# Two transformer blocks on one core: the turn of neighbourhood probabilities one round later, with four probability buffers

## The reference

```
o_a = _gqa_blocked(q_a, k_a, v_a) * jax.nn.silu(g_a)
o_b = _neighbourhood_attn(q_b, k_b, v_b, na_rpb[l])
o_b = o_b * jax.nn.silu(g_b)
mixed = jnp.concatenate([o_a, o_b], axis=-1)
x = x + mixed @ w_out[l]
...
sc = jnp.where(mask, sc + bias.astype(jnp.float32), -jnp.inf)
p = jax.nn.softmax(sc, axis=(-2, -1)).astype(v.dtype)
o = jnp.einsum('bhjqkc,bkjchd->bjqhd', p, v_band)
```

## Time and profile before

| | |
|---|---|
| median of three executions | 2462.85 us (2457.55 to 2464.51) |
| the profiled execution's own time | 2464.41 us |
| its span, first to last instruction | 2462.4 us |
| PE busy | 2380.6 us, 97% |
| DVE busy | 1711.4 us, 70% |
| ACT busy | 1122.1 us, 46% |
| POOL busy | 523.2 us, 21% |
| A steps (first to last `exp` of kind A) | 2043.3 to 2216.5 us |
| B steps (first to last `exp` of kind B) | 2218.9 to 2351.5 us |

### The profile page before, as it was taken

How to read it: one execution, slowest core, us unless ns; L and a number is a source line. 1 busy time by engine, 2 the same in 40 slices (tenths; PEclk the granted TensorE clock), 3 DMA queues, 4 the chain that set the end, 5 groups by cost and what they waited for, 6 DMA issues and landing times.

```text
span 2462.4 us, 32578 instructions
## 1 busy us (share of the span) xinstructions
PE 2380.6 (97%) x11129; PEld 1925.2 (78%) x11129; DVE 1711.4 (70%) x2762; ACT 1122.1 (46%) x1950; POOL 523.2 (21%) x453
## 2 busy tenths in 40 slices
PE   7999999899999999999999899999999999999998
PEld 2578888688878888878888688888888897886677
DVE  7788877788786664277766877785641227998863
ACT  3455455444434223245455544342421127887851
POOL 0211001333232000210100432320110003557731
PEclk9999999999999999999999999998999999999999
DMA  8726665654434731235643754440453472336521
GB/s 322 274 90 212 231 215 200 232 184 154 134 102 142 265 111 75 97 115 181 208 167 116 268 186 126 156 129 18 173 141 122 150 184 73 98 97 171 154 69 69
DMA packets 272970, 382.23 MB, mean 155 GB/s; under 512 B 63665, under 2 KB 173361, under 8 KB 272818
## 3 DMA queue, kind: packets, MB, share of 16 engines
q1 hardware_dynamic: 272818, 380.27, 47.3%
HBM read 279.54 MB, written 106.70 MB: 157 GB/s over the span
## 4 chain that ended last, share of the span: by engine, by line
PE 80%; DVE 9%; issue 5%; POOL 3%; ACT 2%; SPq 1%; DMA 1%; DVEq 0%; POOLq 0%; ACTq 0%
PE banks L2761 22%; PE banks L2762 22%; PE banks L2763 22%; PE banks L2831 2%; PE banks L3307 2%; PE banks L3325 2%; POOL probs L1492 1%; DVE neg_max L2698 1%; DVE stage L2060 1%; PE banks L2779 1%; POOL X L1524 1%; PE banks L3294 1%; PE banks L3295 1%; SPq L1303 1%; DVE X L2437 1%
## 5 line engine op out<-in xcount | busy, mean ns | idle before, releaser
L2761 PE MATMUL banks<-Hhi,Whi 128*128 128x512 f32 x1760 | 696.4, 396 | 25.1 <-DVE X L2437 13.9
L2762 PE MATMUL banks<-Hlo,Whi 128*128 128x512 f32 x1760 | 687.6, 391 | 0.0
L2763 PE MATMUL banks<-Hhi,Wlo 128*128 128x512 f32 x1760 | 687.5, 391 | 0.0
L2761 PEld LDWEIGHTS banks<-Hhi,Whi 128*128 128x128 f32 x1760 | 332.1, 189 | 106.7 <-issue 24.3
L2762 PEld LDWEIGHTS banks<-Hlo,Whi 128*128 128x128 f32 x1760 | 332.3, 189 | 69.9 <-issue 2.4
L2763 PEld LDWEIGHTS banks<-Hhi,Wlo 128*128 128x128 f32 x1760 | 331.9, 189 | 70.3
L2761 PE MATMUL banks<-T,Whi 128*128 128x512 f32 x720 | 283.7, 394 | 6.7 <-DVE Wlo L2353 6.7
L2763 PE MATMUL banks<-T,Wlo 128*128 128x512 f32 x720 | 283.0, 393 | 0.0
L2762 PE MATMUL banks<-T,Whi 128*128 128x512 f32 x720 | 283.0, 393 | 0.0
L1696 ACT ACTIVATE Whi<-stage 128x512 fp32r<-128x512 f32 (+2 forms) x180 | 104.9, 584 | 229.4 <-PE banks L2763 229.2
L2437 DVE SCALAR_TENSOR_TENSOR X<-banks,mod,X 128x512 f32<-128x512 f32 x180 | 134.3, 746 | 98.9 <-PE banks L2763 97.5
(11 more groups left out here) (258 smaller groups left out, 4082.1 us busy)
## 6 DMA issues: line engine op xcount, KB each, us to landing
stage<-w SPq DMA_DIRECT2D x58, 1024.0 KB, 6.4
stage<-hidden SPq DMA_DIRECT2D x224, 256.0 KB, 3.6
hidden<-slot SPq DMA_DIRECT2D x196, 256.0 KB, 2.1
stage<-ada_t SPq DMA_DIRECT2D x36, 1024.0 KB, 5.3
x_saved<-X SPq DMA_DIRECT2D x32, 512.0 KB, 4.5
stage<-w_in SPq DMA_DIRECT2D x13, 1024.0 KB, 6.2
stage<-ada_w SPq DMA_DIRECT2D x12, 1024.0 KB, 7.3
X<-x_saved SPq DMA_DIRECT2D x24, 512.0 KB, 4.9
```

The lines of the kernel that those rows point to most:

```text
L2761: nc.tensor.matmul(out_bank, whi, xhi, start=start, stop=False, skip_group_check=onto)
L2762: nc.tensor.matmul(out_bank, whi, xlo, start=False, stop=False, skip_group_check=onto)
L2763: return nc.tensor.matmul(out_bank, wlo, xhi, start=False, stop=stop, skip_group_check=onto)
```

## The change

In the B steps, `turn` and everything behind it (`probs_hi`, `probs_lo`, `outputs`, `lower_half`, `whole_output`, `gated`) works one round later; `delayed` gives the tile. Kind A keeps its lags. At the change from A to B, round 3 has no turn. B's probabilities get four buffers, `near_probs`, so that `exp` of tile u waits for the turn of u-4; the pads behind them are zeroed four times and not twice. In B, DVE takes `row_maxima` ahead of `invert_sum`. The mask's thirds move from rounds 5, 6, 7 to 3, 6, 7 and, within B, from 13, 14, 15 to 12, 14, 15. `OT` becomes two buffers behind the two biases, `biased` moves behind the new buffers, and `attend_end` writes out the longer tail. SP's code is unchanged.

```diff
-    SC = sb("biased", [P, 2, NI], at=t_at + 8 * S)
     PE_ = sb("probs", [P, 2, S], at=t_at)
+    PB = sb("near_probs", [P, 4, NI + HD], at=t_at)
+    SC = sb("biased", [P, 2, NI], at=t_at + 16 * (NI + HD))
...
+    def delayed(u, lag, kind, before):
+        old, new = u - lag - (before == "B"), u - lag - (kind == "B")
+        return ([(old, before)] if before and old < 0 else []) + ([(new, kind)] if new >= 0 else [])
...
+    def freed(u, kind, first):
+        if kind == "B":
+            return (-2 if u == 0 else 0) if first and u < 4 else 2 * u - 6
+        return 2 * u - 2
...
-                    if kind == "B" and u in (5, 6, 7):
-                        mask_bias(T, 1, u - 5)
-                    if (kind == "B") != last and u in (13, 14, 15):
-                        mask_bias(T, 0, u - 13, ahead=1)
-                    for w, k in lagged(u, 9, kind, before):
+                    if kind == "B" and u in (3, 6, 7):
+                        mask_bias(T, 1, (3, 6, 7).index(u))
+                    rounds = (12, 14, 15) if kind == "B" else (13, 14, 15)
+                    if (kind == "B") != last and u in rounds:
+                        mask_bias(T, 0, rounds.index(u), ahead=1)
+                    for w, k in delayed(u, 9, kind, before):
...
-                reach(act, t_ready, T("v2", 2 * u - 2))
+                reach(act, t_ready, T("v2", freed(u, kind, first)))
...
-                    for w, k in lagged(u, 8, kind, before):
+                    for w, k in delayed(u, 8, kind, before):
                         if w % 4 == 3:
                             lower_half(T, w // 4)
-                    for w, k in lagged(u, 3, kind, before):
+                    for w, k in delayed(u, 3, kind, before):
                         probs_hi(T, w, k)
...
-                    for w, k in lagged(u, 2, kind, before):
-                        invert_sum(T, w)
+                    if kind == "A":
+                        for w, k in lagged(u, 2, kind, before):
+                            invert_sum(T, w)
                     for w, k in lagged(u, 1, kind, before):
                         row_maxima(T, w, k, width(k, w))
-                    for w, k in lagged(u, 3, kind, before):
+                    if kind == "B":
+                        for w, k in lagged(u, 2, kind, before):
+                            invert_sum(T, w)
+                    for w, k in delayed(u, 3, kind, before):
                         probs_lo(T, w, k)
...
-                    for w, k in lagged(u, 3, kind, before):
+                    for w, k in delayed(u, 3, kind, before):
-                        turn(T, w, k, zeroed=w + 1 if kind == "B" and before == "A" and 0 <= w < 2 else 0)
+                        turn(T, w, k, zeroed=w + 1 if kind == "B" and before == "A" and 0 <= w < 4 else 0)
                     scores(T, u, kind, width(kind, u), before)
-                    for w, k in lagged(u, 7, kind, before):
+                    for w, k in delayed(u, 7, kind, before):
                         outputs(T, w, k, zeroed=6 * (w // 4 + 1) if kind == "B" and before == "A" and 0 <= w < 8 else 0)
```

More of the change, by code:

```diff
@@ L395, in build @@
     PTl = sb("PTl", [P, 2, QT, H], F32R, at=h_at + 4 * KT * S)
-    OT = sb("OT", [P, 2, H], at=acc_at - 7 * S // 2)
+    OT = [sb(f"OT{i}", [P, H], at=w_at + 4 * UNIT * (spare + 2 * i) + 4 * (NF + NI)) for i in range(2)]
     OS = sb("OS", [P, 2, H], at=acc_at + S // 2)
@@ L1490, in scale @@
                 pool.sem_inc(sums_seen, 1)
-                row = PE_[:, u % 2, 0:width(kind, u)]
+                row = probs(u, kind)[:, 0:width(kind, u)]
                 nc.gpsimd.tensor_scalar(out=row, in0=row, scalar1=rden[:, u % 4:u % 4 + 1], scalar2=1.0,
@@ L1527, in attend @@
                 for u in range(PAIR):
-                    if u % 4 == 1:
-                        reach(pool, mixed_done, T("vg", (u - 9) // 4))
+                    for w, k in delayed(u, 10, kind, before):
+                        if w % 4 == 3:
+                            reach(pool, mixed_done, T("vg", w // 4 + 1))
                     for w, k in lagged(u, 2, kind, before):
                         scale(T, w, k)
-                    if kind == "B" and before == "A" and u < 2:
+                    if kind == "B" and before == "A" and u < 4:
                         zero_pad(T, u)
@@ L1980, in silu, with exp @@
                         vals(T, 0, P, P, range(4 * i, 4 * i + 4))
-            def exp(T, u, kind, n):
+            def exp(T, u, kind, n, first=False):
                 act.wait_ge(max_done, T("v", u + 1))
-                reach(act, t_ready, T("v2", 2 * u - 2))
+                reach(act, t_ready, T("v2", freed(u, kind, first)))
                 scores = SB_[:, 2 * (u % 2):2 * (u % 2) + 2, :].rearrange("p b n -> p (b n)")[:, 0:n]
@@ L1987, in exp @@
                     scores = SC[:, u % 2, 0:n]
-                nc.scalar.activation(PE_[:, u % 2, 0:n], scores, ACT.Exp, bias=neg_max[:, u % 4:u % 4 + 1],
+                nc.scalar.activation(probs(u, kind)[:, 0:n], scores, ACT.Exp, bias=neg_max[:, u % 4:u % 4 + 1],
                                      scale=-1.0 if kind == "B" else 1.0,
@@ L2003, in lower_half @@
                 reach(act, os_done, T("vg", g - 1))
-                nc.scalar.activation(OT[0:HD, g % 2, :], OB[HD:P, g % 2, :], ACT.Copy).then_inc(ot_done, 1)
+                nc.scalar.activation(OT[g % 2][0:HD, :], OB[HD:P, g % 2, :], ACT.Copy).then_inc(ot_done, 1)
             def attend(T, kind, i, before, last):
                 for u in range(PAIR):
-                    for w, k in lagged(u, 8, kind, before):
+                    for w, k in delayed(u, 8, kind, before):
                         if w % 4 == 3:
                             lower_half(T, w // 4)
-                    for w, k in lagged(u, 3, kind, before):
+                    for w, k in delayed(u, 3, kind, before):
                         probs_hi(T, w, k)
                     for w, k in lagged(u, 1, kind, before):
-                        exp(T, w, k, width(k, w))
+                        exp(T, w, k, width(k, w), before == "A")
             def attend_end(T):
+                lower_half(T, -3)
+                probs_hi(T, -4, "B")
+                exp(T, -1, "B", width("B", -1))
                 probs_hi(T, -3, "B")
-                exp(T, -1, "B", width("B", -1))
                 probs_hi(T, -2, "B")
@@ L3315, in outputs @@
                 if w % QT == 0:
-                    pe.wait_ge(v_loaded[e], raw_loaded + T.loads(16))
+                    pe.wait_ge(v_loaded[e], raw_loaded + T.loads(16, ahead=-1 if w < 0 else 0))
                 if part_of == 0:
@@ L3342, in attend_end @@
             def attend_end(T):
-                for w in range(-7, 0):
+                for w in range(-8, 0):
                     if w < -4:
```

21 lines of the change are left out of this document (13 added, 8 removed).

## The result

The changed kernel takes **2476.6 us** (median of 6 executions, 2471.5 to 2478.3) against 2464.3 us for the kernel before (6 executions of the same comparison): a ratio of 1.0045, 95% interval 1.0035 to 1.0056. It is slower by more than the 0.3% that a measurement of this kernel can tell. The forecast said slower, and 2472.4 us.

A forecast was written before the change was run, and what follows sets the result against it. B rounds were taken as bound by a ring over ACT and DVE, with POOL's lateness reaching PE's turn. Terms -2.3 (B0), +0.9 (tail), +5.9 (mask), +5.1 (clock) summed to +9.6: median 2472.4 us, range 2460 to 2481.

The forecast's parts named there:

- The free round: B rounds without waits: 1.83 us each on PE and DVE, 87.8 instead of 98.6 for 48 rounds, -10.8 us.
- both rings: B rounds' loops over ACT and DVE (exp, reciprocal, maxima, next exp: 2.0 us) and through POOL's scaling to PE's turn.
- B0: First B step: the extra round spares POOL pauses between its scalings, -2.3 us, ends 0 and -3.4.
- Its loads for B1 just fit: Claim that the loads B0 issues for B1 land in time; no cost was put on them.
- The mask's first third: POOL in rounds 3 and 12 waits for the bias load, delaying PE's turns: +5.9 us in place of -10.8.
- The clock: PE after three idle holes of 4.1 us runs at lower clock, 1.7 us lost each: +5.1 us.
- the slow round lies inside the next chain: B steps: low-clock rounds delay the next chain of loads, since VT waits for their outputs; part of the clock's +5.1.
- Tail: Behind the last scores: one more turn and quarter of outputs, +0.9 us, ends 0 and 1.7.
- What would show it: Signs in B1 to B3: POOL mask waits, PE idle stretches, clock under 1.00, rounds of 1.8 us between holes.
- Three idle stretches near 4 us: Sign on PE in the B steps: three such stretches, ended by POOL's scaling of tile 2, lower clock behind them.
- the waits are hidden: Rival, B steps: bias lands within 10.3 us of round 15's scores, so the change is faster, 2450.6 us; chance 0.18.
- Full clock: Rival, PE in the B steps: holes come but the clock does not drop, no change, 2467.3 us; chance 0.20.

The follow-up runs named there:

- the bias first: The changed kernel with SP issuing the bias load ahead of QS, KH, KL and V of the same head: 2452.4 us, ratio to before 0.9954.
- early masks and bias first: The kernel before with mask thirds in the change's rounds and SP's bias load ahead of the head's other loads: 2467.9 us, ratio 1.0016.
- the same order of loads and the old DVE order: The changed kernel with the bias load issued first and DVE's reciprocal put back ahead of the row maxima: 2459.3 us, ratio to before 0.9975.
- masks in rounds 6, 7, 8: The changed kernel with the second head's mask thirds in rounds 6, 7, 8 in place of 3, 6, 7: 2467.5 us, ratio to before 1.0009.
- the change with the old DVE order: The changed kernel, its loads unaltered, with DVE's reciprocal put back ahead of the row maxima: 2474.3 us, ratio to before 1.0046.
- VT behind: The changed kernel with each B-step VT load issued behind QS, KH, KL and bias of the other head: 2458.8 us, ratio to before 0.9979.
- before, early masks: The kernel before with only the mask's first thirds moved, to rounds 3 and 12 from 5 and 13: 2488.0 us, ratio 1.0099.

## Why the prediction was right, and where it was off

The direction, the mechanism and the place were right; the time, 2472.4 against 2476.6, was 4.2 us too low. Term by term, against the profiled executions (predicted +9.6, measured +12.6 in the span):

- **The free round, 1.83 us.** With the load's wait removed it is 1.90 (91.12 / 48). Mis-sized by 4%: in a group of four rounds I had one above 1.67; in the runs it is two, the one with the OS of 2.1 to 2.35 and one beside it of 1.9 to 2.1. The reason I gave was too simple. "With the maxima ahead of the reciprocal and four buffers, both rings are cut" fails as it stands: four buffers alone change nothing, and the maxima ahead alone lose 7.6 us of the 48 rounds. It is the later turn that cuts, and it makes the order on DVE useful.
- **B0, -2.3.** From round 0 to round 15, 34.30 before, 32.63 after: -1.7. With the bias first it is 31.60; the mask for B1 in B0's round 12 waited 2.98 us, which I had held safe ("Its loads for B1 just fit"). Another 0.4 of gain lies ahead of round 0. That means nothing: the start of round 0 lies anywhere between 2211.9 and 2218.3 in the profiled executions of this study.
- **The mask's first third, +5.9 in place of -10.8.** The step that decided, and it held. VT to bias landed was to be 13.0: the five starts of the mask less their VT issues give 12.8, 13.6, 12.9, 12.4, 13.5, mean 13.0. Round 15 to round 6 was to be 16.9: 16.84, 18.55, 17.62. Round 7 to round 15 was to be 16.9: 17.94, 17.36.
- **The clock, +5.1.** I counted three drops of 1.7 us, behind the holes of round 6, and three came, but that the count fits is luck: they stood behind 2.31 (round 15), 3.91 and 3.54 us, and none behind 2.56. The one behind 3.91 us was also longer than the others (0.53 over 2302 to 2308), so the mean of 0.94 over 111.57 us is 6.7 us of PE time at full speed, not 5.1. That "the slow round lies inside the next chain" was right as well: the two VT loads that were issued in slow rounds came 2.65 and 2.35 us behind their scores, the others 1.4 to 1.6.
- Free part, mask and clock together: the 48 rounds grew by 13.0 where 11.0 was predicted. Of the 2.0, B3's last half alone is 1.2 (15.87 against 14.64); the rest can't be told apart from the clock, whose slow stretches lie inside the chains.
- **Tail, +0.9.** From the last scores to the end of the span 114.1 before, 115.8 after: +1.7, the far end of my bound. The kernels with four buffers whose turn isn't later have 115.0; the one with two buffers, early masks and bias first has 114.1. So 0.9 comes with something that all kernels with four buffers share and that I had not priced, and 0.8 with the later turn. They share the layout (OT lies in the weights' space, and DVE has a wait for the last OS behind it); that this is the 0.9 is argued and was not run alone.
- **What would show it.** POOL's waits of up to 5 us in rounds 3 and 2 to 4 in round 12: seen (4.1, 5.4, 5.4 and 3.0, 4.4, 3.4). "Three idle stretches near 4 us": two were (3.91 and 3.54), the first was 2.56. DVE's wait for `exp` at the reciprocal is gone, as forecast.
- **A row read loosely.** The 13.2 us that the prediction puts down to "PE's turns" waiting for POOL is the row of PEld, the turns' weight loads; the row of their matmuls is 6.4 us. No term of the sum rests on it.

Of the rivals, *the waits are hidden* gave 2450.6 us. It is what the kernel becomes once the bias goes first, 2452.4. The rule cited there, that of the Trainium skill, "Perfetto Trace Analysis", section "Optimization Strategy", says that consistent bubbles on the engine that should be full can mean too few buffers. Here buffers were not the cure: with the loads and masks the same, the 48 rounds took 100.52 us with two and 100.53 with four. *Full clock* is out by the 0.94.

## What to carry to other kernels

A step moved earlier on an in-order engine brings its own waits with it, and everything queued behind it pays: before moving one, put the landing of what it waits for beside the new start, and if it doesn't fit, move the load up in its queue first; here one load moved up in SP's order, at two places, turned +0.45% into -0.46%. Parts of a schedule are not worth something one by one: the same swap on one engine gained 4.3 us, gained nothing, or lost 7.6, depending on which chain was longest. And where a step moves later, count the rounds between producer and consumer in each ring, since the ring is divided by that number; more buffers only make room for it, and gained nothing alone.

## What the runs showed of the hardware that I had not expected

- **How long a load takes depends on its place.** The 736 KB bias load took 7.4 to 8.7 us to land as the last of a burst, and, over the eight loads of each kernel, 4.4 to 5.2 us in the kernel before with the bias first, and 4.9 to 7.4 in the change with the bias first, where only the VT load stands ahead of it. I had priced the position by the issue alone. The place isn't all of it: with the same order of loads and the old DVE order, min, median and max were 4.9, 6.7 and 7.8 us.
- **The length of an idle stretch doesn't tell whether PE's clock falls.** Stretches of 1.98 us, 2.00 (masks in rounds 6, 7, 8), 2.05 (the change with the old DVE order) and 2.31 us had the lower clock behind them. Stretches of 1.80 us, 2.03 (VT behind), 2.56 (the change) and even 3.42 us (before, early masks) had not. These runs don't settle what decides. The window behind the 2.03, in the kernel with VT behind:

```profile
2328.00:2334.00 6.00, 5.99 (x34) 4.63 (x35) 4.58 (x15) 5.39 (x14) 5.68 (x6) 1.00 0.14 37
```

and in the kernel before with early masks, the turn behind the 3.42 us, in B2, and the window behind it:

```profile
2303.90 0.76 PE L3308 MATMUL banks<-const,probs 128*128 128x128 f32 x5 [3.42 <-POOL probs L1492]
2304.00:2310.00 6.00, 5.46 (x32) 4.23 (x32) 4.27 (x14) 4.58 (x12) 5.06 (x6) 1.00 0.03 9
```
